# Latent attention and its output projection: two stages put into one, with the products of finished head pairs between the attention steps

## The reference

```
def mla_mixer(u, pos, w_in, q_norm_g, w_q_up, kv_norm_g, w_kv_up, w_out):
    c_q, c_kv, k_rope = split(u @ w_in, [384, 640])
    q  = (rms_norm(c_q, q_norm_g) @ w_q_up).reshape(b, s, 16, 64 + 32)      # 16 heads
    kv = (rms_norm(c_kv, kv_norm_g) @ w_kv_up).reshape(b, s, 16, 64 + 64)
    q, k = (rope on the last 32 columns), v = kv[..., 64:]
    logits = einsum('bqhd,bshd->bhqs', q, k) * 96 ** -0.5
    p = softmax(where(visible, logits, -1e30))
    out = einsum('bhqs,bshd->bqhd', p, v)                                   # 256 x 1024
    return out @ w_out                                                     # 1024 x 1024
...
x = layer_norm(ALPHA * x + (1 + gate) * mla_mixer(x * (1 + scale) + shift, ...), ln_g, ln_b)
```

## Time and profile before

| | us |
|---|---|
| median of 3 runs | 1565.59 (1559.78 to 1573.0) |
| the profiled execution | 1564.0 |
| its span | 1562.2 |
| PE, PEld, DVE, ACT busy, share of the span | 92%, 80%, 74%, 54% |
| mean granted PE clock | 0.976 |

### The profile page before, as it was taken

One profiled execution on the slowest core, in us unless ns is written; L12 is line 12 of the kernel. 1 busy time (PEld: TensorE's weight loads), 2 busy tenths in 40 slices (PEclk: granted clock), 3 DMA queues, 4 the chain that ended last, 5 costly groups with the idle time before them and its releaser, 6 DMA issues. The chain is left out here.

```text
span 1562.2 us, 23401 instructions
## 1 busy us (share of the span) xinstructions
PE 1443.9 (92%) x8807; PEld 1243.0 (80%) x8807; DVE 1157.0 (74%) x2067; ACT 847.6 (54%) x1612; POOL 0.2 (0%) x4
## 2 busy tenths in 40 slices
PE   3999998997989999989999898899997999999888
PEld 3888888996868888878887885788886988788766
DVE  6888788877679987798888666886668557636564
ACT  2545445553456454475444566655455666746663
POOL 0000000000000000000000000000000000000000
PEclk9999999998999999999999999999998999999999
DMA  9999876640046898559887151495555264445200
GB/s 370 352 314 343 302 232 219 213 136 1 1 148 239 290 341 293 198 198 327 295 294 247 57 196 41 151 314 196 196 181 170 87 218 160 111 139 160 80 1 28
DMA packets 197382, 306.16 MB, mean 196 GB/s; under 512 B 10551, under 2 KB 158998, under 8 KB 197270
## 3 DMA queue, kind: packets, MB, share of 16 engines
q1 hardware_dynamic: 196464, 304.40, 57.1%
q10 hardware_dynamic: 806, 0.26, 0.1%
HBM read 303.59 MB, written 1.05 MB: 195 GB/s over the span
## 5 line engine op out<-in xcount | busy, mean ns | idle before, releaser
L915 PE MATMUL bank<-u_hi_lo,w_hi 128*128 128x512 f32 x1344 | 472.7, 396 | 10.2 <-DVE arena L981 10.2
L914 PE MATMUL bank<-u_hi_lo,w_lo 128*128 128x256 f32 x1176 | 327.9, 279 | 0.0
L970 DVE TENSOR_TENSOR w_lo<-weight_ring,w_hi 128x1024 fp32r<-128x1024 f32 x264 | 308.0, 1219 | 17.8 <-ACT w_hi L940 17.1
L915 PEld LDWEIGHTS bank<-u_hi_lo,w_hi 128*128 128x128 f32 x1344 | 246.1, 188 | 62.7 <-DVE arena L981 14.5
L940 ACT CAST w_hi<-weight_ring 128x1024 fp32r<-128x1024 f32 x264 | 260.5, 1047 | 39.9 <-DMA weight_ring<-in_ffn_w_gate_dram 26.9
L914 PEld LDWEIGHTS bank<-u_hi_lo,w_lo 128*128 128x128 f32 x1176 | 221.7, 189 | 7.3
L837 PE MATMUL bank<-src_hi,wp_hi 128*128 128x256 f32 (+2 forms) x672 | 192.7, 301 | 2.2 <-ACT src_hi L434 1.7
L837 PE MATMUL bank<-src_hi,wp_lo 128*128 128x256 f32 (+2 forms) x672 | 181.8, 285 | 0.0
L837 PE MATMUL bank<-src_lo,wp_hi 128*128 128x256 f32 (+2 forms) x672 | 181.5, 285 | 0.0
L353 DVE SCALAR_TENSOR_TENSOR zT<-weight_ring,silu_c,zT 128x1024 f32<-128x1024 f32 x126 | 161.6, 1282 | 4.6 <-DMA weight_ring<-in_mod_w_dram 1.8
L2964 DVE TENSOR_TENSOR wp_lo<-weight_ring,wp_hi 128x1024 fp32r<-128x1024 f32 (+1 forms) x79 | 94.6, 1213 | 74.1 <-ACT wp_hi L2933 73.9
(11 more groups left out here) (382 smaller groups left out, 2308.7 us busy)
## 6 DMA issues: line engine op xcount, KB each, us to landing
weight_ring<-in_mod_w_dram SPq DMA_DIRECT2D x72, 1024.0 KB, 7.0
weight_ring<-in_ffn_w_gate_dram SPq DMA_DIRECT2D x44, 1024.0 KB, 5.9
weight_ring<-in_ffn_w_up_dram SPq DMA_DIRECT2D x44, 1024.0 KB, 5.5
weight_ring<-in_ffn_w_down_dram SPq DMA_DIRECT2D x44, 1024.0 KB, 8.4
weight_ring<-in_hyb_w_in_dram SPq DMA_DIRECT2D x16, 1024.0 KB, 8.2
weight_ring<-in_w_in_e_dram SPq DMA_DIRECT2D x16, 1024.0 KB, 8.0
weight_ring<-in_w_in_o_dram SPq DMA_DIRECT2D x13, 1024.0 KB, 5.2
weight_ring<-in_hyb_w_out_dram SPq DMA_DIRECT2D x4, 1024.0 KB, 5.0
```

The source lines that it names most:

```text
L914: nc.tensor.matmul(bank[:, 0:SEQ], w[1], u[:, 0:SEQ], start=False, stop=False, skip_group_check=True)
L915: last = nc.tensor.matmul(bank[:, :], w[0], u, start=kt == 0, stop=kt == KT - 1, skip_group_check=True)
L970: nc.vector.tensor_tensor(part_view(wl, n, part), raw, part_view(wh, n, part).bitcast(F32), ALU.subtract).then_inc(w_lo.sem, w_lo.up())
```

## The change

`attention` and `out_proj` are no longer called by `mla`. In their place stands one stage, `attend_and_project`, on a `Steps` object with 8 pairs (16 units, 20 steps) and `wide` = 99, so that all logits go to banks 0 and 1 and the logits of unit i wait for the scores of unit i - 1. Transposes have bank 6 alone, so those of unit u wait for ACT's copy of unit u - 1. The products go to banks 2 to 5, as before. The class `Steps` is moved up in the file and gets one more argument (where the turned probabilities lie).

```
-            attention([Pair(heads[2 * p:2 * p + 2], same_bias(bias), uT[:, p, :], causal=False) for p in range(8)])
-            out_proj(D["mla_w_out"][0], uT, 0, x_rows_of=(3, 1))
+            steps = Steps([Pair(heads[2 * p:2 * p + 2], same_bias(bias), uT[:, p, :], causal=False) for p in range(8)], 99, (),
+                          arena.take(2 * 4 * SEQ))
+            attend_and_project(steps, D["mla_w_out"][0], 3)
...
+        def attend_and_project(steps, w_out, rows_of):
+            tiles = [rows_tile(w_out, 2 * m * P) for m in range(n_out)]
+            x_rows = ln_rows(rows_of)
+            first_at = (8, 12, 16, 20)
+            parts_at = {first_at[m] + 2 * k + a: (m, k, a) for m in range(2) for k in range(2) for a in range(TT)}
+            parts_at.update({16: (2, 0, 0), 18: (2, 1, 0), 20: (3, 0, 0), 21: (3, 1, 0)})
+            split_at = {2: 0, 3: 1, 4: 2, 5: 3, 11: 4, 13: 5, 15: 6, 17: 7}
+            scale_at = {10: 0, 14: 1}
+            mix_of = {i - 1: m for m, i in enumerate(first_at)}
...
+            # ACT
+                for i in range(steps.count):
+                    steps.act(act, i)
+                    if i in split_at:
+                        split_hi(split_at[i])
+                    if i in mix_of:
+                        m = mix_of[i]
+                        act.wait_ge(out_taken.sem, out_taken.base + 2 * m + 2)
+                        nc.scalar.copy(mh[:, 2 * m:2 * m + 2, :], uT[:, 2 * m:2 * m + 2, :]).then_inc(mix_hi.sem, mix_hi.up())
...
+            # DVE
+                for i in range(steps.count):
+                    steps.dve(dve, i)
+                    if i - 1 in split_at:
+                        split_lo(split_at[i - 1])
+                    if i in scale_at:
+                        scale_rows(dve, x_rows, scale_at[i])
+                    if i in mix_of:
+                        m = mix_of[i]
+                        dve.wait_ge(mix_hi.sem, mix_hi.base + m + 1)
+                        nc.vector.tensor_tensor(ml[:, 2 * m:2 * m + 2, :], uT[:, 2 * m:2 * m + 2, :],
...
+            # PE
+                for i in range(steps.count + 2):
+                    if i in parts_at:
+                        m, k, a = parts_at[i]
+                        if k + a == 0:
+                            pe.wait_ge(mix_lo.sem, mix_lo.base + m + 1)
+                        if a == 0:
+                            pe.wait_ge(w_lo.sem, w_lo.base + 2 * m + k + 1)
+                        for h in range(2):
+                            last = part(m, k, a, h)
...
+                    if i < steps.count:
+                        steps.pe(pe, i)
+                for h in range(2):
+                    for m in (2, 3):
+                        for k in range(2):
+                            last = part(m, k, 1, h)
```

More of the change, by code:

```diff
@@ L2699, in mla @@
                      for h in range(16)]
-            attention([Pair(heads[2 * p:2 * p + 2], same_bias(bias), uT[:, p, :], causal=False) for p in range(8)])
-            out_proj(D["mla_w_out"][0], uT, 0, x_rows_of=(3, 1))
+            top = arena.at
+            arena.at = keep
+            steps = Steps([Pair(heads[2 * p:2 * p + 2], same_bias(bias), uT[:, p, :], causal=False) for p in range(8)], 99, (),
+                          arena.take(2 * 4 * SEQ))
+            arena.at = top
+            attend_and_project(steps, D["mla_w_out"][0], 3)
             arena.at = base
```

342 lines of the change are left out of this document (194 added, 148 removed).

## The result

| | before | changed |
|---|---|---|
| median, us | 1564.98 (1559.78 to 1573.0, 4 runs) | 1586.33 (1584.05 to 1592.87, 4 runs) |
| ratio | | 1.0139, 95% interval 1.0106 to 1.0172 |
| profiled execution, its span, us | 1564.0, 1562.2 | 1587.49, 1585.4 |
| mean granted PE clock | 0.976 | 0.968 |

The changed kernel is 21.4 us slower, 1.4%. In the profiled executions the difference is 23.5 us; 22.5 us of it lie in the stage, from the first logits to the last product: 83.55 us instead of 61.01 us.

A forecast was written before the change was run, and what follows sets the result against it. Both stages were taken as bound or nearly bound by PE, so the merge could win only 6.1 us of waits. 1564.0 + 12.3 (stops and waits, net) + 6.8 (clock) = 1583.1 us, range 1570 to 1593 us.

The forecast's parts named there:

- sum without the clock: Merged stage at full clock: all stop, wait and fill terms together, +12.3 us, 73.3 us instead of 61.0 us.
- rival C: Every stop ends in a 6.8 us clock fall: 1586.5 us, up to 1592 us; chance 0.15.
- Items 1 and 2: First steps: one pair of logits banks, +1.0 us; uncovered bank and ACT copy waits in steps 3 to 7, +2.2 us.
- Items 3, 4, 5 and 7: PE waits for mixes at steps 8, 12, 16 and the last: +3.5, +4.3, +5.4 and +1.95 us.
- Item 6: Between the stops from unit 8 on, products fill PE's waits of the old attention and stage border: -6.1 us.
- Item 8: Moved low parts, scalings, class and ring order, with the next FFN's loads, cost or gain nothing.
- Item 9: Granted clock falls behind the three new stops, two short and one long: +6.8 us, bounds 0 to 10.2 us.
- The fall behind the old stage: The 6.8 us clock fall after the old stage; its staying away would give 3.4 us, reaching 1560 us.
- Rival B: Mixes are ready when PE reaches them, so the merge pays or costs nothing: 1563.7 us, or 1560 us; chance 0.12.
- Rival A: The stops come but the clock holds: 1576.3 us; chance 0.20.

The follow-up runs named there:

- mix_hi first: Changed kernel with ACT's cast of the attention output (mix_hi) ahead of the weight cast in the same step; one profiled execution, 1586.77 us.
- scaling moved: Changed kernel with DVE's two scalings of x one step earlier (steps 9 and 13 instead of 10 and 14); one profiled execution, 1581.7 us.
- two pairs of banks: Changed kernel with logits of units 1, 3, 5 and 7 in a second pair of banks; 1585.59 us, ratio 1.0126. Its filled version: 1576.58 us, 1.0078.
- the best layout: Changed kernel with parts later, two logits bank pairs below unit 8, first three mix_lo a step later, x scaling a step earlier; 1564.85 us, ratio 1.0005.
- three stops filled: Changed kernel with 5, 7 and 7 repeated, unread logits on PE ahead of the first three mix waits; 1582.52 us, ratio 1.0123.
- the steps alone: Changed kernel's attention form kept, but the projection again its own stage behind it, weight casts too; 1574.73 us, ratio 1.0066.
- late parts: Changed kernel with PE's parts of mixes 0, 1 and 2 at steps 10 to 19, two steps later; 1569.44 us, ratio 1.0045.

## Why the prediction was right, step by step

It was right in sign and size: 1583.1 us predicted, 1586.33 us measured, within 1570 to 1593 us. In the profiled executions 19.1 us more were predicted and 23.5 us came. The sum without the clock held. The clock term was too small: each of the three stops had a long fall, which is rival C's condition (1586.5 us, chance 0.15) and not the forecast's.

- **Items 1 and 2**, the first steps: +3.2 us predicted. The turn of step 7 starts 956.37 - 938.85 = 17.5 us into the stage; before it was 953.49 - 939.59 = 13.9 us: +3.6 us. The third logits too waited, 0.87 us. Of this 1.6 us are the banks; that ACT's copies are the rest is read from its timeline alone.
- **Items 3, 4, 5 and 7**, the four stops: 3.5, 4.3, 5.4 and 1.95 us predicted; 3.35, 4.29, 5.36 and 1.86 us measured as idle time. The prediction counted from start to start; counted so, with 0.4 us for the turn ahead as in item 3, they are 3.6, 4.5, 5.6 and 1.9 us. Their causes were each taken away: PE's place in the list (all stops go), the weight cast (0.8 us at steps 12 and 16, none at 8), the scaling (1.16 us at step 16, 0.09 us at step 12).
- **Item 6**, the waits filled: right for the changed kernel; behind step 8 PE waits only in front of mixes. But it held the merge against the old attention. The new form has more waits to fill, as the run without the merge shows, and the parts fill those too.
- **Item 8**, at nothing: nothing waits for a transfer in the next FFN.
- **Sum without the clock**: 12.3 us. The idle time grew by 12.3 us. That the two agree to the tenth is luck: taking the clock from the windows gives 13.0 us. (Lost there: 6.75 x 0.43 + 6.80 x 0.43 + 5.80 x 0.41 + 3.40 x 0.39 = 9.5 us; 22.5 - 9.5 = 13.0.) The terms as measured from start to start give 3.6 + 15.6 - 6.1 = 13.1 us, nearly the same.
- **Item 9**, the clock, is the term that was mis-sized: 6.8 us from two short falls and one long, where three long ones and one short came, 8.7 us by the busy time at full clock and 9.5 us by the windows. The 10.2 us by which PE was busy longer is the upper bound. The rows of before had one gap of each sort, too few to choose by. The four profiles with stops of this kind, and no filler in them, show more (stop at step 8, 12 and 16, and how long PE's clock was at the lower level behind each):

| | step 8 | step 12 | step 16 |
|---|---|---|---|
| changed | 3.35: 6.8 | 4.29: 6.8 | 5.36: 6.8 |
| mix_hi first | 3.34: 6.8 | 3.48: 3.4 | 4.54: 6.8 |
| scaling moved | 3.35: 3.4 | 4.20: 6.8 | 4.20: 6.8 |
| two pairs of banks | 3.34: 3.4 | 4.29: 6.8 | 5.36: 6.8 |

All seven stops of 4.2 us or more had a long fall. Those near 3.4 us had either, and which one is not a matter of the kernel alone: the stop at step 8 has the same length and the same chain in all four. So two long falls could be counted on and the third was open. The stop behind the last mix, 1.86 us, had a fall of 3.4 us in all four; it was not in the term and cost 1.6 us (nine starts of matmuls in 1017.36 - 1013.72 = 3.64 us instead of 9 x 0.227 = 2.04 us).

- **The fall behind the old stage**, which rival B counted at 3.4 us if it stayed away, is gone in the profiled execution but gives back 1.0 us, since PE waits for ACT there once it is fast; the two late falls take more.

All four stops were followed by a fall. That is the rule of the Trainium skill ("TensorE: Matmul & The Clock Gate", HAM oscillation), that bursts parted by waits pay each time; its case is a wait for a DMA, here PE waits for DVE, and the trace agrees, four times of four. The rule of the Trainium skill ("Perfetto Trace Analysis", optimization strategy) that interleaving regimes may improve performance speaks of regimes in which different engines are the most contended. Here that is PE in both. As the change was laid out the stage grew by 22.5 us, and in the best layout it gave 1.8 us of 61.3 us.

**Rival B** needed some 3.5 us of PE's work between the pair's output and the part. With two steps more (a pair of steps takes 4.3 to 5.0 us) the waits for mix_lo went to 0.28 us, so its condition was right and the changed order did not meet it. The two layouts that met it came to 1569.4 and 1564.9 us, near its 1563.7 us and not below the kernel before. **Rival A** fell: the clock did not hold.

## What to carry to other kernels

Before work of one stage is put between the steps of another, lay the in-order lists beside each other and ask what the put-in instruction waits for: if that hangs on the instruction just ahead of it on the same engine, it stops everything, and two places later it may cost nothing. Count the half clock with a stop on PE: here each of twelve stops of 3.3 to 5.4 us, in four profiles, had a fall behind it, which in the changed kernel put some 9 us on 13 us of stops and waits. Waits that a merge can fill have to be counted against the form that the merge needs (its banks, its copies), not only against the old one.

## What the runs showed of the hardware that was not expected

- Falls of the clock did not come only at the long gaps. Six profiles have waits of 0.98 and 0.87 us ahead of the second and third logits, with the same instructions there. Three of them fell in these steps (that with three stops filled for 6.8 us, the scaling moved and the steps alone for 10.2 us), three ran them at 1.00 (changed, late parts, mix_hi first). The three profiles with two pairs of banks, which do not have these two waits, ran there at 1.00. What decides it from execution to execution stays open.
- A fall can begin inside the gap: the window of the stop at step 8 has a mean clock of 0.85 with no matmul in it, and the first matmul behind it takes 0.80 us instead of 0.50 us.
- Repeated matmuls whose values nobody reads kept the clock at 1.00 through a stage of 73.7 us with the same dependences, and gave 9.0 us back between medians although they overran one mix by 1.0 us.
- The same stop is not always followed by the same fall: behind that at step 8, 3.34 or 3.35 us long, the lower level lasted 6.8 us in two profiles and 3.4 us in two.
